# Layer 1's mixer as one stage of head pairs on chip

## The reference

```python
def mix_odd(h, w_in, w_out, sinks, q_norm, w_uq, kv_norm, w_ukv):
    qc, kc, vc, c_q, c_kv, k_rope = split_cols(h @ w_in, L1_IN_SIZES)   # 512, 128, 128, 384, 256, 32 columns
    o_c = swa_sink_attention(qc, kc, vc, sinks)
    o_d = mla(c_q, c_kv, k_rope, q_norm, w_uq, kv_norm, w_ukv)
    return jnp.concatenate([o_c, o_d], axis=-1) @ w_out
```

## Time and profile before

| | us |
|---|---|
| median of 3 runs | 4772.64 |
| profiled execution, its own time | 4774.24 |
| its span, first to last instruction | 4772.4 |
| TensorE busy in the span | 3671.9 (77%) |
| VectorE busy | 2136.7 (45%) |
| ScalarE busy | 1257.9 (26%) |
| GpSimd busy | 1340.0 (28%) |
| mean granted clock of TensorE | 0.878 |

### The profile page before, as it was taken

One profiled execution on the slowest core, in us unless ns is written; L12 is line 12 of the kernel. 1 busy time (PEld: TensorE's weight loads), 2 busy tenths in 40 slices (PEclk: granted clock), 3 DMA queues, 4 the chain that ended last, 5 costly groups with the idle time before them and its releaser, 6 DMA issues. The chain is left out here.

```text
span 4772.4 us, 80743 instructions
## 1 busy us (share of the span) xinstructions
PE 3671.9 (77%) x31270; PEld 2589.8 (54%) x31270; DVE 2136.7 (45%) x4235; ACT 1257.9 (26%) x2674; POOL 1340.0 (28%) x978
## 2 busy tenths in 40 slices
PE   7869987776698969978677873776899994567784
PEld 6647765444576758767222221662798984422221
DVE  3547644454666333565100003742888884510002
ACT  2433313222332232212111111112455552211111
POOL 3434433200333524363100001330544442400000
PEclk9879998858799979988788986898899997778887
DMA  3125431223354212133699994344222223479996
GB/s 115 32 67 176 176 102 61 73 63 87 106 182 148 98 59 64 60 136 142 272 421 421 421 421 186 102 139 170 63 63 63 63 63 97 157 321 422 421 421 272
DMA packets 330775, 826.54 MB, mean 173 GB/s; under 512 B 117508, under 2 KB 174292, under 8 KB 270580
## 3 DMA queue, kind: packets, MB, share of 16 engines
q1 hardware_dynamic: 321932, 793.69, 45.9%
q0 software_dynamic: 8560, 28.85, 1.7%
HBM read 738.42 MB, written 84.02 MB: 172 GB/s over the span
## 5 line engine op out<-in xcount | busy, mean ns | idle before, releaser
L1305 DVE SCALAR_TENSOR_TENSOR f_ada<-first_hT,condition,f_ada 128x256 f32 (+1 forms) x672 | 287.1, 500 | 0.0
L2169 PE MATMUL moe0e_p_g<-moe_ring,moe0e_xT 128*64 128x512 f32 x608 | 172.9, 648 | 18.0 <-ACT moe0e_xT L2207 9.6
L2671 POOL TENSOR_TENSOR scan_off<-scan_pairs,scan_join 128x256 f32<-128x256 f32 x240 | 185.7, 810 | 0.0
L2935 PE MATMUL scan_bank<-scan_T,scan_off 64*64 64x64 f32 x3840 | 160.6, 222 | 31.8 <-issue 26.5
L343 POOL TENSOR_TENSOR gmi_w_lo<-gmi_w,gmi_w_hi 128x512 fp32r<-128x512 f32 x64 | 122.3, 1912 | 198.2 <-ACT gmi_w_hi L374 198.2
L2137 POOL DMA_INDIRECT moe0e_xg<-moe_h,moe0e_rows x19 | 17.8, 939 | 556.2 <-DMA moe0e_rows<-moe_table 550.2
L2169 PE MATMUL moe0e_p_u<-moe_ring,moe0e_xT 128*64 128x512 f32 x608 | 167.4, 629 | 0.0
L343 POOL TENSOR_TENSOR p_w_lo<-p_w,p_w_hi 128x512 fp32r<-128x512 f32 (+3 forms) x88 | 112.9, 1284 | 175.9 <-ACT p_w_hi L374 175.8
L1266 POOL TENSOR_TENSOR f1u_w_lo<-f1u_w,f1u_w_hi 128x1024 fp32r<-128x1024 f32 x44 | 108.3, 2482 | 192.0 <-ACT f1u_w_hi L1275 192.0
L1266 POOL TENSOR_TENSOR f0u_w_lo<-f0u_w,f0u_w_hi 128x1024 fp32r<-128x1024 f32 x44 | 108.6, 2489 | 190.7 <-ACT f0u_w_hi L1275 190.7
L2935 PEld LDWEIGHTS scan_bank<-scan_T,scan_off 64*64 64x64 f32 x3840 | 137.8, 136 | 40.5 <-issue 33.6
(11 more groups left out here) (711 smaller groups left out, 10541.1 us busy)
## 6 DMA issues: line engine op xcount, KB each, us to landing
moe_ring<-in_moe_w_gu_dram SPq DMA_DIRECT2D x280, 1024.0 KB, 20.8
moe_ring<-in_moe_w_down_dram SPq DMA_DIRECT2D x140, 1024.0 KB, 22.0
first_hT<-in_ada_w_dram SPq DMA_DIRECT2D x48, 1024.0 KB, 7.3
f0u_w<-in_ffn_w_gate_up_dram SPq DMA_DIRECT2D x22, 1024.0 KB, 4.9
f1u_w<-in_ffn_w_gate_up_dram SPq DMA_DIRECT2D x22, 1024.0 KB, 4.9
gmi_w<-in_ga_w_in_dram SPq DMA_DIRECT2D x64, 256.0 KB, 2.7
p_w<-in_ab_w_in_dram SPq DMA_DIRECT2D x48, 256.0 KB, 2.7
f0d_w<-in_ffn_w_down_dram SPq DMA_DIRECT2D x44, 256.0 KB, 2.7
```

The lines of the kernel that those rows point to most:

```text
L1305: ins = nc.vector.scalar_tensor_tensor(out=dst, in0=src, scalar=cond[:, k, which:which + 1], in1=dst, op0=ALU.mult, op1=ALU.add)
L2169: mm = nc.tensor.matmul(p[r, :], xT[:, kd, r], ring[:, s, half, k, g * HID:(g + 1) * HID], start=(kd == 0), stop=(kd == KD - 1), skip_grou ...
L2671: nc.gpsimd.tensor_tensor(off[n][:], strict(u, g), over4(join[:, l + 1, :]), ALU.mult).then_inc(s["off_ready"], 1)
L2935: mm = nc.tensor.matmul(out[r], lhsT[r], rhs[r], start=start, stop=stop, skip_group_check=True)
```

## The change

`attention`, `mla_heads` and `mix_out` are removed. `odd_mixer` takes their place, between p1 and `mix_project`. Nothing of the mixer goes through memory between p1 and the output. Columns of cd_w_in, rows of cd_w_out and columns of the latent weights are put in another order on the host, so that heads h and h+4 (which use different key heads) make a sliding pair, and plain, rotated and half-swapped rotated query channels lie together. w_uq has 1024 columns in place of 768, since the rotated channels stand twice (as they are, and with halves swapped), so that a rotation is two products with tables and one sum.

`odd_mixer` has 32 pair-units: 16 sliding (4 pairs by 4 blocks; one or two blocks of keys) and 16 latent (1 to 4 blocks of keys). Between the units' steps, from slot 9 to slot 30, TensorE has one piece of preparation a slot: 5 turns of the normed c_q and c_kv, one of k_rope, 8 products for plain queries and keys, 4 for rotated queries, 4 for values, each over 2 or 3 slices of 128. The sink is one more column of the bias (L1082's form, 257 wide). All tables, and w_uq and w_ukv, are loaded during p1, whose jobs now are 512 (`vq`), 288 (`kvr`), 512, 128 columns, with no stores.

```diff
-        jobs = [dict(w=w[:, 0:512], mode="F", ..., stores=[(qk_c[0:8].rearrange(two, u=2), qkc[:, 0:4])]),
-                dict(w=w[:, 512:640], mode="F", ..., stores=[(qk_c[8:10].rearrange(two, u=2), qkc[:, 4:5])]),
-                dict(w=w[:, 640:1152], mode="T", ..., stores=[(v_c.rearrange("(t p) c -> p t c", p=P), vq[:, :, 0:128])]),
-                dict(w=w[:, 1152:1440], mode="T", ...)]
-        project_split(nc, "p1", hT[:, :, 0:SEQ], SEQ, jobs)
-        norm_transpose(nc, "nq", ...); norm_transpose(nc, "nkv", ...)
-        project(nc, "uq", ...); project(nc, "ukv", ...)
-        mla_heads(nc, "mh", S, q, kv, kvr[:, :, 256:288], a["cos"], a["sin"], qT_d, kT_d, v_d)
-    attention(nc, "at1", ...); attention(nc, "at2", ...)
-    mix_out(nc, "mo1", S, x_tiles, hT, mixed, a["cd_w_out"], a["norm_mix_post"][1])
+        tables = Tables(nc, "odd_tables", [(bias[:, :, 0:2 * P], a["swa_bias"]), (sink_rows[:], a["swa_sinks"].partition_broadcast(P)), (causal[:], a["causal"]),
+                                           (ropeF[:], a["rope_by_channel"]), (ropeT[:], a["rope_by_token"])]
+                        + [(w_uq[:, k, :], a["mla_w_uq"][k * P:(k + 1) * P, :]) for k in range(3)]
+                        + [(w_ukv[:, k, :], a["mla_w_ukv"][k * P:(k + 1) * P, :]) for k in range(2)], 8)
+        project_split(nc, "p1", hT[:, :, 0:SEQ], SEQ, jobs, fetch=tables)
+        odd_mixer(nc, "om", S, qkc, vq, kvr, w_uq, w_ukv, bias, sink_rows, causal, ropeF, ropeT, c["mla_q_norm"], c["mla_kv_norm"], hT)
+    mix_project(nc, "mo1", S, x_tiles, hT, a["cd_w_out"], a["norm_mix_post"][1])
```

The core of `odd_mixer` (u is the head of the pair, m the slot):

```diff
+    PREP = [(TURN, c) for c in range(5)] + [(KPE, 0), (QN, 0), (KN, 0), (X0, 0), (X1, 0)] + [(V, t) for t in range(NT)]
+    PREP += [(QN, 1), (KN, 1), (QN, 2), (KN, 2), (X0, 1), (X1, 1), (QN, 3), (KN, 3)]
+    FIRST = 9
...
+                    for u in range(2):
+                        nc.tensor.matmul(ps_s[u][:, 0:w], qn[half(u), hp, rows], kn[half(u), hp, 0:w], start=True, stop=False, skip_group_check=True)
+                    for u in range(2):
+                        h = 2 * hp + u
+                        r = slice(32 * (h % 4), 32 * (h % 4) + 32)
+                        mm = nc.tensor.matmul(ps_s[u][:, 0:w], qpe[r, h // 4, rows], kpeT[r, 0:w], start=False, stop=True, skip_group_check=True)
...
+                for m in range(SLOTS):
+                    x, u = m // 2, m % 2
+                    if u == 0 and x + 2 < UNITS:
+                        scores(x + 2)
+                    if u == 0 and 1 <= x <= UNITS:
+                        weigh(x - 1)
+                    if u == 1 and x < UNITS:
+                        turn(x, 0)
+                        turn(x, 1)
+                    if 0 <= m - FIRST < len(PREP):
...
+                        elif kind == KN:
+                            for k in range(2):
+                                mm = nc.tensor.matmul(bank[:], w_ukv[:, k, n * P:(n + 1) * P], cT[:, 3 + k, :], start=(k == 0), stop=(k == 1))
+                        elif kind == V:
+                            for k in range(2):
+                                mm = nc.tensor.matmul(bank[:], cT[:, 3 + k, n * P:(n + 1) * P], w_ukv[:, k, 512:1024], start=(k == 0), stop=(k == 1))
+                        else:
+                            c0 = {QN: 0, X0: 512, X1: 768}[kind] + n * P
+                            for k in range(3):
+                                mm = nc.tensor.matmul(bank[:], w_uq[:, k, c0:c0 + P], cT[:, k, :], start=(k == 0), stop=(k == 2))
...
+                    if m < NT:
+                        squares.step(nc.scalar.activation(junk[:], cq[:, m, :], ACT.Square, accum_out=ss[:, 0, m:m + 1]))
+                        squares.step(nc.scalar.activation(junk[:, 0:256], ckv[:, m, :], ACT.Square, accum_out=ss[:, 1, m:m + 1]))
...
+                for m in range(SLOTS):
+                    x, u = m // 2, m % 2
+                    if x + 2 < UNITS:
+                        biggest(x + 2, u)
+                    if u == 1 and x < UNITS:
+                        dve.wait_ge(turned[0], x + 1)
+                        w = unit(x)[3]
+                        nc.vector.tensor_copy(probsT[0][x % 2][:, 0:w], ps_t[0][:, 0:w]).then_inc(turned_copied[0], 1)
+                    if u == 0 and x + 1 < UNITS:
+                        invert(x + 1)
+                    if NT + 1 <= m < 2 * NT + 1:
+                        t = m - NT - 1
+                        dve.wait_ge(rstd_step, 3)
+                        nc.vector.tensor_scalar(cq[:, t, :], cq[:, t, :], rstd[:, 0, t:t + 1], None, ALU.mult).then_inc(normed, 1)
+                        nc.vector.tensor_scalar(ckv[:, t, :], ckv[:, t, :], rstd[:, 1, t:t + 1], None, ALU.mult).then_inc(normed, 1)
```

More of the change, by code:

```diff
@@ L814, in attention_tables @@
         "dil_bias": np.ascontiguousarray(np.stack(dil, 1)),
-        "swa_rel": np.where(swa, delta, BIG).astype(f),
-        "zero_extra": np.zeros((P, 4 * P), f),
+        "swa_bias": np.ascontiguousarray(np.stack([np.where(swa, delta, BIG).astype(f) * f(-4.0 * 0.5 ** h) for h in range(8)], 1)[:, :, 2 * P:]),
         "causal": np.where(delta >= 0, 0.0, -BIG).astype(f),
@@ L1372, in _ @@
             @block.gpsimd
             def _(pool):
-                for t in range(NT):
-                    nc.gpsimd.tensor_copy(kk[:, t, :, 0:D_NOPE], kv4[:, t, :, 0:D_NOPE]).then_inc(pool_step, 1)
-            def empty(which, engine, eng, g):
-                eng.wait_ge(turned, g + 1)
-                if g >= 4:
-                    eng.wait_ge(stored[g % 4], 16 * (g // 4))
-                if which == "act":
-                    engine.activation(outT[g % 4][:], tp[g % 4][:], ACT.Copy).then_inc(emptied[0], 1)
-                else:
-                    engine.tensor_copy(outT[g % 4][:], tp[g % 4][:]).then_inc(emptied[1], 1)
@@ L1415, in _, with normalise @@
-            @block.scalar
-            def _(act):
-                for g in range(0, G, 2):
-                    empty("act", nc.scalar, act, g)
-            @block.tensor
-            def _(pe):
-                pe.wait_ge(dve_step, ROTATED)
-                pe.wait_ge(pool_step, NT)
-                for g in range(G):
-                    if g >= 4:
-                        pe.wait_ge(emptied[g % 2], (g - 4) // 2 + 1)
-                    src = q4 if g < D_HEADS else kk
-                    for t in range(NT):
-                        mm = nc.tensor.transpose(tp[g % 4][:, t * P:(t + 1) * P], src[:, t, g % D_HEADS, :], S.ident[:, :])
-                    mm.then_inc(turned, 1)
+                def normalise(n, u):
+                    pair, b, k0, w, lo = unit(n)
+                    pool.wait_ge(den_turned, n + 1)
+                    nc.gpsimd.tensor_tensor(probs[u][n % 3][:, lo:lo + w], probs[u][n % 3][:, lo:lo + w], rden[:, n, u:u + 1].broadcast_to([P, w]), ALU.mult).then_inc(probs_ready, 1)
@@ L1498, in first_block @@
         at += w
-    mixed = dram(nc, "mixed0", [SEQ, D])
     norm_transpose(nc, "n0", S, x_tiles, hT, cols=[(c["norm_mix_pre"][:, 0:KD], None)] * NT)
@@ L1546, in first_block @@
-        project(nc, "ukv", ckvT, SEQ, [dict(w=a["mla_w_ukv"][:, 512 * n:512 * n + 512], mode="T",
-                                            epi=copy_to(lambda j, n0, n=n: kv[:, j, 512 * n:512 * n + 512])) for n in range(2)])
-        mla_heads(nc, "mh", S, q, kv, kvr[:, :, 256:288], a["cos"], a["sin"], qT_d, kT_d, v_d)
-    attention(nc, "at1", S, qk_c[0:8], qk_c[8:10], v_c, mixed[:, 0:512], 8, HD, HD ** -0.5, 1, group=4,
-              slope0=-4.0, rel=a["swa_rel"], extra=a["zero_extra"], sinks=a["swa_sinks"])
```

482 lines of the change are left out of this document (233 added, 249 removed).

## The result

The kernel after took 4613.9 us (median of 4, 4607.18 to 4616.98) where the kernel before took 4770.3 in the runs beside it (median of 4, 4759.08 to 4774.93): a ratio of 0.9674, 95% interval 0.9653 to 0.9694, so 156 us less. The range of 4610 to 4676 holds it; the forecast's own range of 4618 to 4660 does not. The sign and 85% of the gain were forecast (136 of 160 us between the two profiled executions), and 24 us more came. The result lies only 4 us inside the lower end of the given range, and nothing in the prediction is worked out to that end (its own forecast stopped at 4618, the packed rival stood at 4605). That the range holds it owes something to luck.

What follows compares the result with a forecast made beforehand. It took hand-overs of one head-unit at a time to bound the old 289.7 us stretch; 0.5 + 147 + 5.1 + 1 = 153.6 us would replace it, giving 4637 us, own range 4618 to 4660, given range 4610 to 4676.

Steps and rivals of the forecast that it cites:

- the packed rival: New stage: TensorE stays packed with work, 115 us for the stage and 4605 in all; chance 0.08.
- fill and units 0 to 4: Start of the new stage: fill 3.5 us, then five units, the first two with squared sums on ScalarE; 22.3 us.
- slots 9 to 14: Three units with five turns of normed rows and one of the rotary key: 3.2 us each, 9.6.
- slots 15 to 30: Eight units with all 40 preparation products, bound by TensorE: 38.6 + 8 x 1.55 = 51.0 us.
- last half unit, latent units, drain: End of the new stage: last half unit 1.6 us, latent units 48.6, drain 6.
- the factor 1.09 on all but 51.0: Layer 0's mixer, 78.1 us measured over 71.6 modelled, applied to 88.1 us where TensorE isn't packed with products.
- tables in the input projection: Table and weight loads during the input projection: between -1.5 and +8 us, taken as +1.
- 7 us of cover: Slots 15 to 30: preparation fills 0.9 us a unit that sliding units would leave idle, 7 us in all.
- the two loops: Unit time is the larger of TensorE's own list and the scores-reductions-reciprocal loop; latent head pair 12.1 us.
- Half clock: Every unit: small products don't raise the clock, about 50 us more, stage 197, total 4687; chance 0.14, whole or part.
- Units that don't overlap: Every unit: turns wait for GpSimd's division, 15 us a unit, 4970 us in all; chance 0.01.
- a preparation out of its place: Preparation products wait for movers and run nearly alone: +7 to +15 us, 4644 to 4652, inside the forecast.

Runs made afterwards that it cites:

- the nine extra products: Kernel after, with one more 128x512 product in each of slots 0 to 8: stage 132.9 us against 129.8, total 4624.6 us.
- The run with both chains out: Kernel after, without layer 0's three gate-logarithm operations and seven chained state updates per head pair: layer 0's mixer 71.2 us against 78.1.

## Why the prediction came out as it did

Term by term, prediction against the kernel after:

| term | forecast | measured | miss |
|---|---|---|---|
| fill and units 0 to 4 | 22.3 | 18.5 | 3.8 |
| slots 9 to 14 | 9.6 | 8.1 | 1.5 |
| slots 15 to 30 | 51.0 | 48.5 | 2.5 |
| last half unit, latent units, drain | 56.2 | 54.7 | 1.5 |
| the factor 1.09 on all but 51.0 | 7.9 | none | 7.9 |
| edges (0.5 + 5.1; 0.67 + 4.85) | 5.6 | 5.5 | 0.1 |
| tables in the input projection | +1 | -0.9 | 1.9 |

These are 19 of the 24 us between 4638 and the profiled execution's 4614.0; 4.6 more lie in later stages and 0.4 ahead of the projection.

**What bounds the stage: right.** Slots 15 to 30 take 48.5 us, with TensorE busy 48.5 of it, at clock 1.00; the products cost 0.91 each (2.74 for three, the six records from 909.51), and the 0.965 of the earlier trace rows had the cold start in it that the prediction named and then did not take off: 40 x 0.055 is 2.2 of the 2.5 us. The prediction's 7 us of cover can't be confirmed: the run without the preparation gives 7 at most, and 5 by estimate.

**The factor: the term that failed.** Without the factor the model was 7 us too long in the 81 us outside slots 15 to 30 (88.1); with it 15 too long. I distrusted it by the wrong stage: layer 0's 78.1 over 71.6 was put down to the form of the units. The timeline of before had those waits named, 5.4 us of the 6.5, and I had the em_state one in the earlier trace rows. The run with both chains out gave 71.2. The 7.9 us that the factor added are a third of the whole miss.

**The latent units: right in sum, off in price.** A pair of score products costs 0.42, 0.64, 0.84 and 1.06 us for 128 to 512 columns. I had 0.27 for 128 (half of the 256-wide one) and 0.53 for 256. The 0.53 of the earlier trace rows was a low case; the same group 16 us earlier in that trace takes 0.63 to the next:

```profile
221.67 0.70 PE L915 MATMUL em_ps_s<-qka 64*128 64x256 f32 x4
222.30 0.88 PE L936 MATMUL em_ps_o<-em_probsT,vrt 128*64 128x128 f32 x12
```

By the measured prices TensorE's list of a head pair comes to 11.6 us, not 10.5. About half of that is the score pairs, the rest turns and weighings, mostly of one and two blocks (a turn 0.37 and 0.65 where I had 0.24 and 0.48). With 0.83 of waits it is 12.45, where the two loops gave 12.1. The other loop came out shorter than estimated, so the two errors nearly cancelled, which is luck: the scores and weighings of three and four blocks stand in no wait at all. The 32-row pair cost what the 64-row pair cost: the lower end of its bounds.

**The start: right in cause, one unit counted too long.** The turns of units 0 to 4 stand at 886.76, 890.53, 894.59, 897.84 and 900.33, the first preparation product at 901.35. So the fill took 3.9 us (forecast 3.5), units 0 and 1 took 7.8 (8.8), units 2 and 3 took 5.7 (6.5), and of unit 4 only 1.0 us had passed (3.5). Slot 9 is that unit's second slot, and its product stands right behind the turn: I had counted the unit whole, and that is 2.5 of the 3.8 us. The squares set units 0 and 1, as the run without them shows, at 2.2 us over what the two units take without them. The prediction priced this part with no half clock, though TensorE had it for 13 of the 18.5 us; what that costs wasn't measured by itself, and the nine extra products raised the clock earlier for a net loss.

**What was costed at nothing: right.** GpSimd's division (0.4 us for 40 us of work), the movers and the rotary key show in no wait of TensorE's products. The tables came in at 0.80 of the DMA in the busiest stretch (830 to 850, 266 GB/s), over the 204 of the earlier trace rows. ScalarE's waits for p_w, in the list of waits of the input projection, were these:

```profile
ACT p_w_hi L374 <- DMA p_w<-in_cd_w_in_dram: 4.3, 2, 3.6
```

Two waits, of 3.59 us before 806.59 and 0.74 before 807.96, both ahead of the first table's load (822.37). So the tables cost ScalarE no wait at all, and the projection as a whole came out 0.9 shorter (78.5 from its first weight load to its last copy, before 79.4). Within -1.5 to +8 I took a value 1.9 too high.

**The rivals.** Packed TensorE (115 us) was nearer than its 0.08 allowed: the measured 129.8 lies between it and 147. Half clock (197) held only in some 13 us at the start and the last 8. The Trainium skill (TensorE: Matmul & The Clock Gate, What's actually happening) ties the clock to sustained activity. The new units agree, with 1.00 while TensorE is busy 15.6 of 19.5 us. The old sliding attention doesn't: its clock stayed at 0.50 with TensorE busy 79 of 106 us, and also through 14.9 us without a single wait (978.98 to 993.90). Drains between forms of 64 and 32 rows, which the Trainium skill (TensorEngine Tiling (Array Packing), Key Properties) speaks of, are not to be seen: the two pairs follow at 0.63 and 0.64. Units that don't overlap, and a preparation out of its place, did not occur.

## What to carry to other kernels

When a like stage is used as a yardstick, list the waits in it by name and leave out those whose cause the new stage lacks, before any ratio is made of it. When a run without some step comes out shorter, look whether TensorE's busy time fell for the same products; that part is the clock and not the step. Take the price of a product from a row without its start or a neighbour's overlap in it, and take a pair's price at each width from its own row. Work that is independent of a chain can stand nearly anywhere beside it if the binding engine's list has waits to fill: here a start at slot 16 or at slot 9 made no difference.

## What the runs showed of the hardware

- Two fp32 score products on 64 or on 32 rows each, side by side, cost 0.42, 0.64, 0.84 and 1.06 us for 128, 256, 384 and 512 columns: 0.21 for the pair and 0.21 for every 128 columns. A single product of 128x512 on 128 rows costs 0.91. By this fit half of the pair's price at 128 columns doesn't depend on the columns.
- The clock rose to 1.00 some 15 to 17 us after the first score group of the paired units, with the preparation (0.64, 0.68, then 1.00 in stretches of ten), without it, and in the sliding units alone (0.56, 0.76, 1.00), and after some 10 us without the squares. The old form of the same work stayed at 0.50 for 106 us, 14.9 of them in a row without a wait. What in the old form keeps it down was not tried.
